# Ten more weight panels split on ScalarE instead of GpSimd in a two-block transformer kernel

## The reference, cut to what matters

```python
for l in range(DEPTH_2):                       # 2 layers
    u = rms_norm_2(h, attn_norm[l])
    proj = jnp.einsum('bsd,dc->bsc', u, w_in[l])       # 1024 x 7424
    (dq, dk, dv, rq, rk, rv, rg, gq, gk, gv, gate_logits) = split_cols(proj, IN_SPLITS)
    lam = exp(sum(lam_q1 * lam_k1)) - exp(sum(lam_q2 * lam_k2)) + lambda_init
    ...                                        # differential attention, retention, grouped attention
    h = h + jnp.einsum('bsd,de->bse', merged, w_out[l])
    m = jnp.square(jax.nn.relu(jnp.einsum('bsd,df->bsf', rms_norm_2(h, mlp_norm[l]), w_mlp_in[l])))
    h = h + jnp.einsum('bsf,fd->bsd', m, w_mlp_out[l])
```

## Time and profile before

| | |
|---|---|
| time, median of 3 runs | 1844.46 us (1844.4 to 1844.8) |
| the profiled execution's own time | 1844.82 us |
| its span, first to last instruction | 1843.0 us |
| TensorE matmul busy | 1813.7 us, 98% |
| VectorE busy | 1261.1 us, 68% |
| ScalarE busy | 516.6 us, 28% |
| GpSimd busy | 515.3 us, 28% |
| mean granted TensorE clock | 0.999 |

### The profile page before, as it was taken

The page is one execution under the profiler, slowest core; times in us unless marked ns, Lnnn a source line. Parts: engine busy times, 40 slices in busy tenths (PEclk is TensorE's granted clock), DMA queues, the critical chain, the costliest instruction groups (busy, mean ns, idle before and its releaser), DMA issues.

```text
span 1843.0 us, 30281 instructions
## 1 busy us (share of the span) xinstructions
PE 1813.7 (98%) x11948; PEld 1619.7 (88%) x11948; DVE 1261.1 (68%) x1662; ACT 516.6 (28%) x842; POOL 515.3 (28%) x574
## 2 busy tenths in 40 slices
PE   7999999999999999999999999999999999999999
PEld 4777777888989888888899999988899999898888
DVE  6657564336267887788598966886666886788665
ACT  3000001013123412322135544432112555442210
POOL 2211211211144014444340002364434000326442
PEclk9999999999999999999999999999999999999999
DMA  9347774221333424455544433445545433345552
GB/s 373 134 157 298 264 269 152 101 91 69 115 138 130 179 76 159 160 182 206 183 171 166 145 138 116 182 171 195 185 180 183 161 140 135 137 161 183 186 202 91
DMA packets 45197, 307.07 MB, mean 167 GB/s; under 512 B 5536, under 2 KB 6048, under 8 KB 8736
## 3 DMA queue, kind: packets, MB, share of 16 engines
q1 hardware_dynamic: 41200, 293.71, 43.7%
q10 hardware_dynamic: 3888, 11.78, 1.8%
HBM read 302.33 MB, written 3.15 MB: 166 GB/s over the span
## 4 chain that ended last, share of the span: by engine, by line
PE 88%; DVE 7%; issue 3%; ACT 1%; DMA 1%; DVEq 0%; ACTq 0%; POOL 0%; POOLq 0%
PE ps L2194 44%; PE ps L2242 12%; PE ps L2282 7%; PE ps L2221 6%; PE ps L2288 4%; DVE wlo L776 4%; PE ps L2869 1%; PE ps L2264 1%; PE ps L2268 1%; PE ps L2265 1%; PE ps L2442 1%; PE ps L2893 1%; PE ps L2879 1%; DVE xparts L862 1%; PE ps L2744 1%
## 5 line engine op out<-in xcount | busy, mean ns | idle before, releaser
L776 DVE TENSOR_TENSOR wlo<-landing,whi 128x1024 fp32r<-128x1024 f32 x482 | 610.4, 1301 | 233.3 <-PE ps L2242 74.9
L2194 PE MATMUL ps<-xparts,whi 128*128 128x256 f32 (+1 forms) x3232 | 495.6, 311 | 3.8 <-ACT xparts L1723 2.1
L2194 PEld LDWEIGHTS ps<-xparts,whi 128*128 128x128 f32 x3232 | 443.7, 192 | 43.1 <-issue 8.0
L691 POOL TENSOR_TENSOR whi<-landing,ones 128x16 fp32r<-128x16 f32 x184 | 89.9, 489 | 1289.4 <-PE ps L2194 717.6
L2194 PE MATMUL ps<-xparts,wlo 128*128 128x256 f32 (+1 forms) x2368 | 346.7, 299 | 2.0 <-DVE wlo L776 2.0
L2194 PEld LDWEIGHTS ps<-xparts,wlo 128*128 128x128 f32 x2368 | 320.0, 191 | 20.3 <-DVE wlo L776 3.0
L693 POOL TENSOR_SCALAR whi<-landing 128x1008 fp32r<-128x1008 f32 x184 | 210.5, 1144 | 0.0
L694 POOL TENSOR_SCALAR whi<-landing 128x1024 fp32r<-128x1024 f32 x184 | 208.8, 1135 | 0.0
L2221 PE MATMUL ps<-xparts,whi 128*128 128x512 f32 x752 | 180.1, 392 | 0.0
L2221 PEld LDWEIGHTS ps<-xparts,whi 128*128 128x128 f32 x752 | 138.4, 188 | 27.0
L2242 PE MATMUL ps<-xparts,whi 128*128 128x256 f32 (+1 forms) x960 | 155.0, 319 | 0.0
(11 more groups left out here) (307 smaller groups left out, 2005.3 us busy)
## 6 DMA issues: line engine op xcount, KB each, us to landing
landing<-in_stream SPq DMA_DIRECT2D x248, 1024.0 KB, 4.8
ws<-in_stream SPq DMA_DIRECT2D x25, 1024.0 KB, 4.9
big<-in_stream SPq DMA_DIRECT2D x4, 1024.0 KB, 5.9
spectra<-big ACTq DMA_DIRECT2D x8, 256.0 KB, 4.3
ws<-spectra ACTq DMA_DIRECT2D x2, 1024.0 KB, 4.8
ws<-in_tabs ACTq DMA_DIRECT2D x1, 1280.0 KB, 7.0
h<-in_xT ACTq DMA_DIRECT2D x1, 1024.0 KB, 5.4
ws<-in_ctxT SPq DMA_DIRECT2D x1, 1024.0 KB, 7.2
```

The lines of the kernel that those rows point to most:

```text
L691: pool.tensor_tensor(hi[:, 0:FIRST], panel[:, 0:FIRST], ones[:, 0:FIRST], ALU.mult)
L776: ins = v.tensor_tensor(wlo[:, s % 2, c], panel[:, c], whi[:, s % 2, c].bitcast(F32), ALU.subtract)
L2194: ins = mm(out, a, b, start=first and opens and k == ks[0], stop=last and k == ks[-1], skip_group_check=True)
```

## The change

`ACT_HIGH` begins with panel 2 instead of panel 7, in both layers. In layer 0 ScalarE makes the high parts of panels 2 and 3 ahead of `first_rms` and those of panel 4 behind it. In layer 1 it makes those of panel 2 ahead of `boundary_rms` and those of panel 3 behind it. All later ones are made in the loop, at step i for panel i + 2: from panel 5 (step 3) in layer 0, and from panel 4 (step 2) in layer 1. GpSimd's list is shorter by these five panels a layer. TensorE and VectorE wait for ScalarE's counter instead of GpSimd's for them.

```diff
-        ACT_HIGH = (*range(7, 29), O_OUT + 2, O_OUT + 3, O_MIN)
+        ACT_HIGH = (*range(2, 29), O_OUT + 2, O_OUT + 3, O_MIN)
...
             for l in range(LAYERS):
                 link[0], link[1] = l, 0
+                ahead = (4, 3)[l]
+                for i in range(2, ahead):
+                    layer_high(l, i)
                 if l == 0:
                     first_rms()
                 else:
                     boundary_rms(2 * l, step)
+                layer_high(l, ahead)
                 act.wait_ge(turned_rstd, l + 1)
                 a.activation(token_rstd[:], ps[:, 1, 0:2 * TT], ACT.Identity).then_inc(token_set, 1)
...
-                    if i + 2 in ACT_HIGH:
+                    if i + 2 > ahead:
                         layer_high(l, i + 2)
                     if i == 0:
                         lam_parts()
...
                         last = panel(g, s, token(opened([ps[:, j, 0:n], ps[:, j, COLS:COLS + n]]), 0, n),
-                                     within=turn_rstd if l == 0 and i == 3 else None,
+                                     made=layer_made(l, i), within=turn_rstd if l == 0 and i == 3 else None,
                                      behind=(lambda: boundary_sums(0)) if l == 0 and i == 2 else None)
```

## The result

The changed kernel takes 1855.46 us (median of 5 runs, 1854.47 to 1856.72) against 1844.8 us for the kernel before beside it (5 runs, 1844.4 to 1846.58). The ratio is 1.0057, 95% interval 1.0045 to 1.0068: 10.7 us lost. The forecast was 1849.1 us with a range up to 1850.4 us; the direction was right, the size was not. The profiled execution took 1856.72 us, with a span of 1854.6 us against 1843.0 us.

The account below looks back on a forecast made before the run. The prediction took TensorE as the bound: -0.46 us (layer 0) + 3.84 (layer 1 stall) + 1.3 (clock) = +4.68 us on the 1844.46 us median, so 1849.1 us, +0.25%. The range was 1847.5 to 1850.4 us.

Parts of the forecast that it names:

- The bound: Whole kernel: TensorE, busy 98% of the span; gains must come from its waits, and new waits are added in full.
- Layer 0's gain: Layer 0 opening: line 1376 starts earlier without GpSimd beside VectorE's low halves, so TensorE's column turn comes 0.46 us earlier.
- VectorE's relief: Rival, both openings: VectorE gains 6.8 us from faster low halves, giving 1841.5 us; chance 0.03.
- Layer 0's cover: Layer 0, ScalarE: the added panels are ready in time, panel 5 by 0.85 us; cost 0.
- The standing in layer 1: Panel 4 of layer 1: TensorE waits for ScalarE's high part, held behind lam_parts' wait for the small product; 3.84 us lost.
- The clock after it: Behind layer 1's stall: TensorE's clock falls to its lower level, costing 1.3 us, between 0 and 1.8 us a fall.
- the 2.07 us standing: Kernel before, around 735 us: TensorE's longest wait, after which its clock fell to 0.50, costing 1.8 us of full speed.
- Two low stretches: Rival, layer 1: a second low clock stretch on half-wide panel 4, or late panel 5; 1.8 us more, 1850.9 us; chance 0.08.
- The clock stays up: Rival, layer 1: the stall comes but the clock does not fall; 1847.8 us, +0.18%; chance 0.15.

Follow-up runs that it names:

- Experiment 5: Changed kernel with panel 4 multiplied at its full width of 256 columns in both layers; 1853.05 us.
- experiment 2: Changed kernel, with layer 0 also making panel 4's high part in the loop at step 2, behind the small product; 1864.86 us.
- experiment 3: Changed kernel, with layer 1 making panel 4's high part directly behind the exponential, ahead of projected(1) and (2); 1853.18 us.
- experiment 6: Changed kernel with panel 4 at full width in both layers and, in layer 1, its high part made ahead of the wait for the small product; 1845.44 us.
- experiment 8: Changed kernel, with ScalarE's lam_parts and its wait moved to step 2, behind panel 4's high part, in both layers; 1845.17 us.
- experiment 4: Changed kernel, layer 1's panel 4 high part made half before the small-product wait, half behind the exponential; 1849.59 us; two added executions 1854.72 and 1852.19 us.
- experiment 1: Changed kernel, with layer 1 making panel 4's high part behind panel 3's, ahead of the wait for the small product; 1844.49 us.

## Why the prediction was wrong, point by point

**The bound.** Right. TensorE's waits were the place to look, and the new wait came in full. Nothing was caught up behind it.

**Layer 0's gain.** 0.46 us forecast, 0.37 measured, in the bounds. VectorE's relief there, 1.70 us a pair, measured 1.69 (2.35 for 4.04), and TensorE itself was late next, as said; its 32 matmuls took 4.10 us to the turn and not the 4.01 taken from layer 1.

**Layer 0's cover.** Right: panel 5's high part was in time, and TensorE has no wait there.

**The standing in layer 1.** Right in place, cause and size: 3.84 us forecast, 3.97 - 0.13 = 3.84 measured. That it agrees to the hundredth is luck: the halves began 0.1 us earlier than in the sum, and TensorE started 0.14 us behind them and not 0.05.

**The clock after it.** This is the step that failed, as the term "I take 1.3 us" with its upper bound of 1.8 us a fall. It measured 4.88 us in panel 4 and 0.97 us in panel 5, 5.85 us. With it the sum is -0.46 + 3.84 + 5.85 = 9.2 us, against the 9.6 of the trace. The mechanism was right: the clock fell, as the 2.07 us standing said. The Trainium skill (page "TensorE: Matmul & The Clock Gate", section "Why this matters for your kernels") has it too, that a long enough gap between bursts of matmuls brings the clock back to its lower level. The trace agrees, with 0.50 at 1412 us in a standing of 3.70 us; the 2.07 us that the prediction put beside this rule is shorter than the gap that the page warns of, so that row goes beyond the page. What was wrong was to take the price from one fall, at 735 us, behind which TensorE worked on matmuls 256 columns wide. Behind the new standing comes the one panel of the layer that is 128 wide. At the high level that panel's pitch (from one matmul's start to the next) is 0.113 us, almost the 0.120 of a full one, so it looked like ordinary work; at the low level its 32 matmuls took 0.214 us each, and its weight loads 0.333 us instead of 0.192:

```profile
L2198 PEld LDWEIGHTS ps<-whi,xparts x28: 333/333/333, 1413.7 to 1419.5; 128*128 128x128 f32 x28
```

(minimum, median and maximum in ns.) Experiment 5 shows the difference that the width makes: 1.8 us of full speed lost instead of 6.8. Why the narrow panel holds the clock down is not shown: TensorE is busy without a gap in it. The 9.2 us are still 1.5 us short of the median's 10.7; 0.3 of them is the wait for line 1605, which the prediction did not have.

**The rivals.** "Two low stretches" named the right doubt, that TensorE "may not earn its clock back at once" on panel 4. It got a chance of 0.08 for want of a row, and its price, 1.8 us more, was well under the 4.6 us by which the term was short. "The clock stays up" did not occur at panel 4 in any profile with 2.3 us or more; behind the 2.07 us at 735 us it did, in 3 of 13 profiles. VectorE's relief came, 10.2 us of busy time over the span, and paid 0.37 us.

**The range.** Its lower end is mis-added: 1844.46 + 3.7 - 0.46 is 1847.7, not 1847.5. Its upper end was too low. It took its upper end from the same single row. A cost that no row shows at this place needed a bound from the longer stretch: the whole of panel 4, 5.4 us, at half speed is 5.4 us more, and 1.8 us for a stretch beyond it; 1844.46 - 0.46 + 3.84 + 5.4 + 1.8 = 1855.0 us would have been the upper end. Even that is 0.4 us under the measured 1855.46; with the prediction's own bounds for the gain (0.29) and the standing (4.1) it is 1855.5. This is an estimate made after the result.

## What to carry to other kernels

An instruction moved to another engine takes over every wait that stands in front of it there; list these, not the engine's idle share. When TensorE is the bound, a new standing costs more than its length: price the fall of its clock by what TensorE does next, and take the whole of a thin stretch at half speed, and a stretch beyond it, as the upper bound (here the clock came back 2 to 5 us into panel 5). If there must be a standing, it was cheaper here in front of wide matmuls than of narrow ones (7.6 against 11.0 us).

## What the runs showed of the hardware

- The clock fell behind standings of 3.70 us (after, experiments 2 and 5) and 2.27 us (experiment 3) in every profile taken. Behind 1.33 us it fell in two of three with the half-wide panel, and not in the one with the full-wide panel. Behind the 2.07 us at about 735 us it fell in 10 of 13 profiles; experiments 6, 8 and the second added execution of experiment 4 kept it.
- The fall needn't come while TensorE stands: in experiment 3 it came 2.6 us behind the restart, in the two executions of experiment 4 some 0.9 and 1.2 us, in experiment 5 some 0.9 us, at 735 us in the kernel before 1.3 us.
- With 128-wide matmuls behind the standing the clock did not come back during the panel, in six of six falls seen: the low stretches are 10.2 or 13.7 us long. With 256-wide ones it came back within it (experiment 5, 3.4 us). The 128-wide panel didn't bring it down by itself, in the kernel before or in experiments 1 and 8.
- A VectorE low half takes 1.2 us alone and 2.0 us beside the instructions of GpSimd at lines 693 and 694 (pairs of 2.35 and 4.04 us at panel 3 of layer 0); where the two overlap only in part, as in layer 1 of the kernel before, a pair took 2.50 to 2.66 us.
- The times of one kernel vary by 2 to 5.6 us (the kernel before 1843.02 to 1848.66). In the profiles the clock costs 0, 1.7 or 3.4 us of full speed in the first 40 us and 0 or 1.7 us at 735 us. A difference of 0.4 us, such as layer 0's, can be seen here only in a trace.
